# Attention on one core: GpSimd's sums of two quads go to VectorE, in a ring of seven slots

## What is computed

```python
def fox_block(q, k, v, fq, fk, q_pos, k_pos):
    s = jnp.einsum('bqhd,bkhd->bhqk', q, k, preferred_element_type=jnp.float32) * ATTN_SCALE
    s = s + (jnp.transpose(fq, (0, 2, 1))[..., :, None] - jnp.transpose(fk, (0, 2, 1))[..., None, :])
    mask = k_pos[None, :] <= q_pos[:, None]
    s = jnp.where(mask[None, None], s, -jnp.inf)
    p = jax.nn.softmax(s, axis=-1)
    return jnp.einsum('bhqk,bkhd->bqhd', p.astype(v.dtype), v)
```

## Time and profile before

| | |
|---|---|
| runs | 3452.81, 3453.6, 3458.11 us; median 3453.6 |
| profiled execution | 3452.1 us, of which the trace's span is 3450.5 |
| mean granted TensorE clock | 0.967 |
| attention's instructions | 1076 to 2442 us |
| busy in the span | PE 94%, PEld 67%, DVE 51%, POOL 40%, ACT 33% |

### The profile page before, as it was taken

How to read it: one execution, slowest core, us unless ns; L and a number is a source line. 1 busy time by engine, 2 the same in 40 slices (tenths; PEclk the granted TensorE clock), 3 DMA queues, 4 the chain that set the end, 5 groups by cost and what they waited for, 6 DMA issues and landing times. The chain is left out here.

```text
span 3450.5 us, 47480 instructions
## 1 busy us (share of the span) xinstructions
PE 3234.9 (94%) x16720; PEld 2314.0 (67%) x16720; DVE 1744.2 (51%) x2947; ACT 1126.3 (33%) x1536; POOL 1383.9 (40%) x1273
## 2 busy tenths in 40 slices
PE   8999999796977999999999999999799999959998
PEld 5777777682734666666666666665488888848886
DVE  4333333262524767676666666666344434444544
ACT  4222222141311455555455555455311211110011
POOL 1000000133332888888888888888400000000000
PEclk9999999898986999999999999999899999979999
DMA  5333334399997113232222323220211111156664
GB/s 181 135 129 128 129 134 148 133 387 365 374 381 177 38 41 84 49 75 60 65 61 63 69 56 71 60 74 10 95 49 61 70 64 49 61 173 207 193 204 146
DMA packets 240077, 435.55 MB, mean 126 GB/s; under 512 B 63588, under 2 KB 107717, under 8 KB 237804
## 3 DMA queue, kind: packets, MB, share of 16 engines
q1 hardware_dynamic: 215403, 358.92, 34.0%
q0 software_dynamic: 20768, 68.17, 5.1%
q10 hardware_dynamic: 3734, 6.28, 0.6%
HBM read 314.39 MB, written 119.08 MB: 126 GB/s over the span
## 5 line engine op out<-in xcount | busy, mean ns | idle before, releaser
L1041 DVE TENSOR_REDUCE at_max_parts<-at_mx 128x1 f32<-128x512 f32 x896 | 612.3, 690 | 166.3 <-PE at_mx L1115 152.4
L978 ACT ACTIVATE at_probs<-at_st,at_gap 128x1024 f32<-128x1024 f32 x448 | 498.8, 1115 | 376.0 <-PE at_st L1143 375.3
L944 POOL TENSOR_TENSOR at_pair_sum<-at_probs 128x1024 f32<-128x1024 f32 x224 | 537.7, 2401 | 140.1 <-ACT at_probs L978 118.2
L1163 PE MATMUL at_o_ps<-at_probs,at_v 128*64 128x512 f32 (+3 forms) x2304 | 490.6, 564 | 0.0
L1163 PEld LDWEIGHTS at_o_ps<-at_probs,at_v 128*64 128x64 f32 x2304 | 179.7, 137 | 261.6 <-issue 219.9
L945 POOL TENSOR_TENSOR at_quad_sum<-at_pair_sum 128x512 f32<-128x512 f32 x224 | 305.8, 1365 | 17.6
L93 PE MATMUL ga_acc<-keep_gate_high,ga_w_high 128*128 128x512 f32 x768 | 299.8, 390 | 0.0
L95 PE MATMUL ga_acc<-keep_gate_high,ga_w_low 128*128 128x512 f32 x768 | 299.8, 390 | 0.0
L94 PE MATMUL ga_acc<-ga_h_low,ga_w_high 128*128 128x512 f32 x768 | 299.5, 390 | 0.0
L1115 PE MATMUL at_mx<-keep_key_one,at_q_top 71*128 71x512 f32 (+2 forms) x576 | 236.0, 416 | 9.9 <-DMA at_q_one<-scratch_q_parts 5.6
L93 PE MATMUL mg_acc<-mg_w_high,mg_mix_high 128*128 128x512 f32 x512 | 201.2, 393 | 46.6 <-DVE mg_mix_low L1769 38.8
(11 more groups left out here) (330 smaller groups left out, 5748.3 us busy)
## 6 DMA issues: line engine op xcount, KB each, us to landing
dc_pages<-in_cache_k_dram SPq DMA_DIRECT2D x128, 256.0 KB, 11.0
dc_pages<-in_cache_k_dram POOLq DMA_DIRECT2D x128, 256.0 KB, 6.1
dc_pages<-in_cache_v_dram SPq DMA_DIRECT2D x128, 256.0 KB, 9.4
dc_pages<-in_cache_v_dram POOLq DMA_DIRECT2D x128, 256.0 KB, 5.6
scratch_h_t<-pj_h_t SPq DMA_DIRECT2D x8, 2048.0 KB
scratch_q_parts<-pj_stage SPq DMA_DIRECT2D x32, 512.0 KB, 3.4
scratch_k_parts<-pj_stage SPq DMA_DIRECT2D x32, 512.0 KB, 2.8
scratch_attn_t<-at_o_out SPq DMA_DIRECT2D x128, 128.0 KB, 2.4
```

Source lines behind the costliest of these rows:

```text
L944: chain.link(nc.gpsimd.tensor_tensor(pair, first, second, ALU.add))
L978: nc.scalar.activation(probs[:, s % RING], st[:, s % 2], ACT.Exp, bias=bias).then_inc(exp_done, 1)
L1041: nc.vector.tensor_reduce(max_parts[:, b % AHEAD, t, c:c + 1], mx[:, n % 2, 0:width], AX_X, ALU.max).then_inc(bank_done, 1)
L1163: last = nc.tensor.matmul(o_ps[half * HD:(half + 1) * HD, b % 2, at:TILE], v[:, h % 2, 4 * c + own], probs[:, s % RING, half, at:TILE], st ...
```

## The change

GpSimd no longer adds two quads' sums. Each quad's sum is kept, in slot n % 7 of the same seven slots, and VectorE adds the sum of each quad, from a block's second on, to that of the quad before: 224 joins instead of 96. GpSimd's 128 additions of L925 go. `join_after` and all other orders stay.

```diff
-    SUMS = 6
+    SUMS = 7
...
-    def summed_with_next(n):
-
-        c = n - quad_base[block_of[n]]
-        return c % 2 == 0 and c < row(block_of[n])
-
-    kept = [n for n in range(NQUAD) if not summed_with_next(n)]
-
     def sum_slot(n):
 
-        return SUMS if summed_with_next(n) else kept.index(n) % SUMS
-
-    joins = [n for n in kept if kept.index(n) and block_of[kept[kept.index(n) - 1]] == block_of[n]]
+        return n % SUMS
+
+    joins = [n for n in range(1, NQUAD) if block_of[n - 1] == block_of[n]]
...
-        quad_sum = m.sb("quad_sum", [P, SUMS + 1, TILE])
+        quad_sum = m.sb("quad_sum", [P, SUMS, TILE])
...
-            def end(n, last):
-
-                if n > quad_base[block_of[n]] and summed_with_next(n - 1):
-                    chain.link(last)
-                    last = nc.gpsimd.tensor_tensor(quad_sum[:, sum_slot(n)], quad_sum[:, sum_slot(n)], quad_sum[:, SUMS], ALU.add)
-                last.then_inc(summed, 1)
-
             def add_quad(n):
...
                 pool.wait_ge(exp_done, 2 * n + 2)
-                if not summed_with_next(n) and kept.index(n) >= SUMS:
-                    old = kept[kept.index(n) - SUMS]
-                    if kept[kept.index(old) + 1] in joins:
-                        pool.wait_ge(joined, joined_by(kept[kept.index(old) + 1]))
+                if n >= SUMS:
+                    old = n - SUMS
+                    if old + 1 in joins:
+                        pool.wait_ge(joined, joined_by(old + 1))
                     else:
                         pool.wait_ge(bank_ready, bank_of["den", block_of[old]] + 1)
...
-                    end(n, nc.gpsimd.tensor_tensor(out, pair[:, 0], pair[:, 1], ALU.add))
+                    nc.gpsimd.tensor_tensor(out, pair[:, 0], pair[:, 1], ALU.add).then_inc(summed, 1)
...
-                end(n, nc.gpsimd.tensor_tensor(out[:, 3 * P:TILE], out[:, 3 * P:TILE], second[:, 1, 3 * P:TILE], ALU.add))
+                nc.gpsimd.tensor_tensor(out[:, 3 * P:TILE], out[:, 3 * P:TILE], second[:, 1, 3 * P:TILE], ALU.add).then_inc(summed, 1)
...
-                before = kept[kept.index(n) - 1]
-                nc.vector.tensor_tensor(quad_sum[:, sum_slot(n)], quad_sum[:, sum_slot(n)], quad_sum[:, sum_slot(before)], ALU.add).then_inc(joined, 1)
+                nc.vector.tensor_tensor(quad_sum[:, sum_slot(n)], quad_sum[:, sum_slot(n)], quad_sum[:, sum_slot(n - 1)], ALU.add).then_inc(joined, 1)
```

## The result

The changed kernel takes 3521.6 us (median of 4 runs, 3511.5 to 3527.0) against 3454.5 us for the kernel before (4 runs, 3452.8 to 3458.1): a ratio of 1.0189, 95% interval 1.0164 to 1.0215. It is 67 us slower, where I had forecast 24.

What follows compares the result with a forecast made beforehand. TensorE's instructions were taken to bound attention. Late totals +24.8, late units +2.8 and the end −3.5 summed to +24.1 us, forecast 3478 us (chance 0.70), range 3464 to 3499 us including the third rival.

Steps and rivals of the forecast that it cites:

- GpSimd's 173 us: GpSimd in attention: 128 additions and the gaps between them go, 173 us, none on the path before the last stages.
- Three joins ahead of a total: Ends of row 4 and 5 blocks: third join meets a pair sum, total 1.55 us late, 16 times, 24.8 us.
- The row-7 ends: Row-7 blocks also end with three joins, the third done about when the total starts: nothing, at most 0.9 us.
- Late units: After stages with three joins and no total, such as stage 9: TensorE's third unit 0.4 us late, seven times, 2.8 us.
- The end: Last total of attention: the last join comes earlier, gain 3.5 us, bounds 2.5 and 4.1.
- Ring of seven: GpSimd's wait before quad n for the join of quad n−6 or the total behind it: costs nothing.
- The lower end of the range: Totals behind row 4 and 5 blocks at 0.9 us late each, 16 times; the range began at +11, 3464 us.
- priced the third join by today's second ones: Rival at row 4 and 5 ends: third join takes 1.57 us, total 0.4 late, 3457 us; chance 0.05.
- Stall: 1.55 us: Stage 5's total, and 16 such places: TensorE waits 1.55 us and cannot win it back, 24.8 us in all.
- TensorE's busy time unchanged: Sign named for the changed kernel's profile: TensorE's busy time stays as before.
- the heavy rival: VectorE late in most stages, all places with three joins cost: +40 us, 3493 us; chance 0.13.
- its top, 3499 us: Upper end of the range: the forecast's own range ended at 3488 us, the VectorE-late rival takes it to 3499.

Runs made afterwards that it cites:

- the version with 208 joins: Kernel before, GpSimd's second sum restricted to the last two quads of blocks of rows 4 and 5, no third joins: 3457.1 us, ratio 1.0004.
- row 4 alone: Kernel before, GpSimd's second sum restricted to row 5's last two quads, so only row 4's eight totals are late: 3491.9 us, ratio 1.0105.
- 13 of 16 at 2.6 us: Kernel before with five unread VectorE reductions ahead of the last join of each row 4 or 5 block, no join added: 3602.5 us, ratio 1.0417.
- two extra matmuls: Changed kernel with two unread matmuls on TensorE ahead of each of the 16 late totals: 3477.7 us, ratio 1.0069 to the kernel before.
- (four): Changed kernel with four unread matmuls on TensorE ahead of each of the 16 late totals: 3479.7 us, ratio 1.0076 to the kernel before.

## Why the prediction was wrong

**The direction and the mechanism of the stalls were right**, and they account for a third of the loss. TensorE bounds attention, and GpSimd's 173 us were worth nothing beside it: right, as the version with 208 joins shows at a ratio of 1.0004. Three joins ahead of a total: right place by place. In stage 5 the third join took 2652 ns (forecast 2.69), the total waited 1.47 us (1.55), and nothing but these 16 totals and the last one waited. The row-7 ends cost nothing, as said: at the one that answers to the earlier trace rows the third join took 0.69 us. Late units: 0.4 us each, as said. The end: 3.2 us for 3.5. Ring of seven: no wait on it can be seen. The lower end of the range, 0.9 us for a late total, was worked out from no row; the waits, 1.45 to 1.56 us, stayed well above it. The rule of the Trainium skill (SBUF — State Buffer, "Who interferes with whom") held at the joins shown, and whoever had priced the third join by today's second ones would have been 1.1 us off at each place.

**The step that failed** is the one that makes a sum of the stalls: "Stall: 1.55 us. TensorE cannot win it back", and under what would show it, "TensorE's busy time unchanged". I took the durations of TensorE's instructions from rows at full clock and let idle gaps into that engine without asking what its clock does behind them; and by that the busy time was off too, 3289.1 us for 3234.9. The term left out is six stages at half clock, 47 us in the profiled execution, twice the stalls themselves. No row of before had such a gap between 1120 and 2380 us: its longest wait in that stretch is 0.42 us, and the one of 1.16 us at 2391 was followed by full clock. But the kernel before had the sign in its own clock records: half-clock stretches in the other phases, and one of 20.5 us that began inside the wait of 7.16 us of the earlier trace rows. I gave VectorE being late in most stages as the heavy rival at +40 us, so the range had a reason to be wide, but the wrong one, and its top, 3499 us, was 23 us short of the median.

The Trainium skill has the rule (TensorE: Matmul & The Clock Gate, "Part 1"): TensorE runs at 2.4 GHz while it is kept busy and is set back to 1.2 GHz after idling. The trace agrees on both levels (granted clock 1.00 and 0.50, 0.24 and 0.43 us between matmuls). The rule of the Trainium skill doesn't give a fall after idle gaps as short as these, and there the runs decide: it came behind 12 of 40 gaps of about 1.5 us. The prediction should have had it as a rival with a price: a stage at half clock costs 7.6 us. How many stages would be hit stood neither in the rows of before nor in the Trainium skill.

**What stays open.** Not every gap of 1.5 us lowers the clock: six of 16 in one execution of the changed kernel, four of 16 in the next, two of eight with row 4 alone, and 13 of 16 at 2.6 us. In both profiles of the changed kernel the affected heads are three apart, and both late totals of a head are hit or neither. That looks like a matter of when a gap falls, but no run here settles it. Nor does any run change what TensorE does ahead of these gaps, which is always the weighting. The varying number of stretches would explain why the time of the changed kernel spreads over 24 us from run to run (3502.6 to 3527.0 in eight runs), where the kernel before spreads over 5 to 10 on a chip.

## What to carry to other kernels

An idle gap in an engine that is the bound can cost more than its length, if the engine is TensorE: price each new wait once as idle time and once as a stage at half clock, with the pitch of the matmuls at either level from rows. Where a short wait can't be avoided, a few matmuls whose result nobody reads can keep the clock up; here two of them at each wait saved 37 us of 61. And an average load says little about moved work: 112 of 128 additions were free in sum, and the loss came from 16 that met a 2.4 us GpSimd instruction in front of something that TensorE waits for.

## What the runs showed of the hardware that was not expected

Gaps of 1.45 to 1.60 us in an otherwise busy TensorE were followed by half clock 10 times in 32 in the changed kernel and twice in 8 with row 4 alone; gaps of 2.5 to 2.7 us by 13 stretches in 16 places; the gap of 1.16 us once in eleven profiles, for 3.4 us; gaps of 0.80 to 0.92 us (two extra matmuls) and of 0.33 to 0.48 us (four) not once in 16 each. In the changed kernel the clock falls not in the gap but 1.5 to 1.9 us after the engine has resumed, and stays down for 17.1 us, once 20.5, though TensorE is busy throughout. Behind the gaps of 2.5 to 2.7 us it falls between 0.2 us before the total starts and 2.1 us after, for 13.7 to 20.5 us.
